# The norm behind the output projection, in two halves of the tokens

## What is computed

```python
x = x + gate[:, None, :] * jnp.einsum("bsd,de->bse", merged, w_out)
x = _rmsnorm(x, final_norm_w)        # x * rsqrt(mean(x*x) + 1e-6) * w

h = x @ pw1_w + pw1_b                # conformer_conv
a, g = jnp.split(h, 2, axis=-1)
h = a * jax.nn.sigmoid(g)
h = causal_dwconv(h, dw_w, dw_b)     # 31 taps for each channel
...
```

## Time and profile before

| | us |
|---|---|
| median of 3 runs (lowest, highest) | 2154.98 (2154.73, 2155.09) |
| the profiled execution, its own time | 2160.05 |
| its span, first to last instruction | 2158.0 |
| TensorE busy in the span | 2031.0 (94%) |
| VectorE busy | 1139.9 (53%) |
| ScalarE busy | 789.9 (37%) |
| GpSimd busy | 37.6 (2%) |

### The profile page before, as it was taken

How to read it: one execution, slowest core, us unless ns; L and a number is a source line. 1 busy time by engine, 2 the same in 40 slices (tenths; PEclk the granted TensorE clock), 3 DMA queues, 4 the chain that set the end, 5 groups by cost and what they waited for, 6 DMA issues and landing times.

```text
span 2158.0 us, 23636 instructions
## 1 busy us (share of the span) xinstructions
PE 2031.0 (94%) x9190; PEld 1621.6 (75%) x9190; DVE 1139.9 (53%) x1330; ACT 789.9 (37%) x1037; POOL 37.6 (2%) x49
## 2 busy tenths in 40 slices
PE   1998999999999899979999999989999999999996
PEld 0874678887688578668888888868777888888885
DVE  6674324225544498776455554354366745555435
ACT  2323233225522465345222232264365452222223
POOL 0000000000000000002000000020000010000000
PEclk8897999999999899989999999999999999999998
DMA  7211122221122111111222223212200222222231
GB/s 320 79 59 39 40 78 98 97 98 40 40 97 98 58 40 58 68 59 59 98 97 97 97 97 113 102 59 98 79 1 3 106 78 97 97 97 97 98 101 55
DMA packets 25861, 177.65 MB, mean 82 GB/s; under 512 B 2752, under 2 KB 4928, under 8 KB 5312
## 3 DMA queue, kind: packets, MB, share of 16 engines
q1 hardware_dynamic: 24064, 160.95, 21.8%
q10 hardware_dynamic: 1728, 15.73, 1.8%
HBM read 174.57 MB, written 2.10 MB: 82 GB/s over the span
## 4 chain that ended last, share of the span: by engine, by line
PE 85%; DVE 7%; ACT 4%; issue 1%; DMA 1%; POOL 0%; DVEq 0%; ACTq 0%; SPq 0%
PE PS L445 23%; PE PS L446 23%; PE PS L447 23%; PE PS L863 2%; PE PS L873 2%; PE PS L513 1%; PE PS L511 1%; PE PS L512 1%; PE PS L522 1%; PE PS L685 1%; DVE ADAS L1421 1%; PE PS L738 1%; DMA SWR<-w_small 1%; PE PS L688 1%; PE PS L719 1%
## 5 line engine op out<-in xcount | busy, mean ns | idle before, releaser
L445 PE MATMUL PS<-H,WH 128*128 128x512 f32 (+1 forms) x1600 | 623.3, 390 | 25.7 <-POOL L L414 12.0
L446 PE MATMUL PS<-L,WH 128*128 128x512 f32 (+1 forms) x1600 | 616.2, 385 | 0.0
L447 PE MATMUL PS<-H,WL 128*128 128x512 f32 (+1 forms) x1600 | 616.0, 385 | 0.0
L1353 DVE TENSOR_TENSOR WL<-RAW,WH 128x2048 fp32r<-128x2048 f32 x145 | 332.2, 2291 | 287.0 <-ACT WH L903 286.6
L445 PEld LDWEIGHTS PS<-H,WH 128*128 128x128 f32 x1600 | 303.5, 190 | 92.6 <-issue 19.7
L903 ACT ACTIVATE WH<-RAW 128x2048 fp32r<-128x2048 f32 x145 | 276.5, 1907 | 224.5 <-PE PS L447 179.2
L447 PEld LDWEIGHTS PS<-H,WL 128*128 128x128 f32 x1600 | 303.2, 189 | 59.9
L446 PEld LDWEIGHTS PS<-L,WH 128*128 128x128 f32 x1600 | 303.5, 190 | 58.8 <-issue 0.8
L445 PE MATMUL PS<-FH,WH 128*128 128x512 f32 (+1 forms) x376 | 142.8, 380 | 0.0
L1238 ACT ACTIVATE TT<-TT 128x512 f32<-128x512 f32 x44 | 27.8, 632 | 310.4 <-DVE TT L1932 310.4
L447 PE MATMUL PS<-FH,WL 128*128 128x512 f32 (+1 forms) x376 | 141.2, 375 | 0.0
(11 more groups left out here) (307 smaller groups left out, 2714.3 us busy)
## 6 DMA issues: line engine op xcount, KB each, us to landing
RAW<-w SPq DMA_DIRECT2D x149, 1024.0 KB, 4.9
ADA<-w_ada ACTq DMA_DIRECT2D x8, 1536.0 KB, 23.5
X<-x_t SPq DMA_DIRECT2D x1, 2048.0 KB, 14.8
PWR<-w_ple ACTq DMA_DIRECT2D x2, 1024.0 KB, 4.9
out<-X SPq DMA_DIRECT2D x8, 256.0 KB, 2.1
PR<-p_t ACTq DMA_DIRECT2D x2, 512.0 KB, 5.8
PAR<-par SPq DMA_DIRECT2D x1, 334.0 KB, 6.7
SWR<-w_small SPq DMA_DIRECT2D x1, 160.0 KB, 18.5
```

The lines of the kernel that those rows point to most:

```text
L445: nc.tensor.matmul(ps, wh, xh, start=start, stop=False, skip_group_check=skip)
L446: nc.tensor.matmul(ps, wh, xl, start=False, stop=False, skip_group_check=skip)
L447: return nc.tensor.matmul(ps, wl, xh, start=False, stop=stop, skip_group_check=skip)
L1353: v.tensor_tensor(WL[:, p], RAW[:, p], WH[:, p].bitcast(F32), ALU.subtract).then_inc(w_lo, 1)
```

## The change

The norm N_FINAL is no longer made on whole rows. `w_out` becomes a `mixed` stage with a `last_slot`, and `pw1` starts with a `first_slot`. In detail:

- During slots 1 to 3 of `w_out`, ScalarE squares the pairs of rows that are complete (`ln_squares`) and VectorE adds the squares into ACC (`squared`).
- The last slot runs tokens 0 to 255, then 256 to 511. Each half is added to X (`w_out_half`), its squares are made (`ln_half_squares`) and summed (`ln_half_sums`), one matmul of 256 columns averages over the partitions (`ln_stats` without the column of means), then come root (`rms_std`), reciprocal (`ln_recip`) and scaling (`rms_scale`) of that half.
- H is copied by pairs of rows and halves of tokens (`rms_hi`); L is made by GpSimd in the loop of L414 in place of VectorE.
- ScalarE splits the weights of `pw1`'s slot 1 between the two halves, no longer behind the norm; `pw1` is called with `split_first=False`. The load of the square root's table stands ahead of the third squaring, under slot 3.
- `LN_AFTER` gets an entry more, so that all five norms share the counters; `SHIFT_OF` and `D0` hold the counts of those that differ. Helpers used by both kinds of norm move up unchanged in what they issue.

```diff
@@ -338,11 +338,13 @@
 
         ADA_PARTS = (1, 0, 2)
 
-        N_X, N_SSM, N_FINAL, N_CONV = range(4)
+        N_X, N_SSM, N_CONV = range(3)
         LN_OF = {N_CONV: 0}
 
 
-        LN_AFTER = {"pw2": 0, "down0": 1, "wo": 2, "down1": 3}
+        LN_AFTER = {"w_out": 0, "pw2": 1, "down0": 2, "wo": 3, "down1": 4}
+        SHIFT_OF = {"pw2": 0, "down0": 1, "wo": 2, "down1": 3}
+        D0 = {"w_out": 0, "pw2": 2, "down0": 5, "wo": 8, "down1": 11}
         NP = KC // 2
         KH = 4
 
...
@@ -406,7 +408,7 @@
             select(M_SSM, ALU.is_ge, NEG, -1, 1)
             select(TRI, ALU.is_ge, 0.0, 1, -1)
 
-            for stage in ("pw2", "down0", "wo"):
+            for stage in ("w_out", "pw2", "down0", "wo"):
                 i = LN_AFTER[stage]
                 for h in range(2):
                     for p in range(NP):
@@ -528,12 +530,16 @@
                                  stop=True).then_inc(mean_ready, 1)
 
             def ln_shift(stage):
-                pe.wait_ge(s01_ready, LN_AFTER[stage] + 1)
+                pe.wait_ge(s01_ready, SHIFT_OF[stage] + 1)
                 nc.tensor.matmul(PS[:, 6, :], PAIRC.to_broadcast([P, P]), S01[:], start=True,
                                  stop=True).then_inc(m0_ps, 1)
 
             def ln_stats(stage, h):
                 pe.wait_ge(st_acc, 2 * LN_AFTER[stage] + h + 1)
+                if stage not in SHIFT_OF:
+                    nc.tensor.matmul(PS[:, 4 + h, HT:T], MEANC.to_broadcast([P, P]), ACC[:, h, 1, :],
+                                     start=True, stop=True).then_inc(lst_ps, 1)
+                    return
                 nc.tensor.matmul(PS[:, 4 + h, :], MEANC.to_broadcast([P, P]), ACC[:, h].rearrange("p a t -> p (a t)"),
                                  start=True, stop=True).then_inc(lst_ps, 1)
 
@@ -579,7 +585,7 @@
 
                 for j in range(COUNT[stage] - 1):
                     slot(Step(j), stage, units, ready if j == 0 else None,
-                         midway=(lambda: ln_shift(stage)) if j == 1 else None)
+                         midway=(lambda: ln_shift(stage)) if j == 1 and stage in SHIFT_OF else None)
                 last_slot(stage, units)
 
             pe.wait_ge(const_ready, 6)
@@ -750,8 +756,7 @@
                     turn(i - 2)
 
             gemm("att_out", ((YH, YLA), hl), (ya_lo, lambda k: k + 1))
-            gemm("w_out", ((MH, ML), (MH, ML)), (mg_lo, lambda k: k + 1))
-            norm(N_FINAL)
+            mixed("w_out", ((MH, ML), (MH, ML)), (mg_lo, lambda k: k + 1))
 
 
             def taps(s, ahead):
@@ -765,9 +770,10 @@
                 mm.then_inc(cp_ps, 1)
 
             def pw1(s):
-                first = isinstance(s.val(), int) and s.val() == 0
-                slot(s, "pw1", (hl, hl), normed(N_FINAL) if first else None)
-                if not first:
+                if isinstance(s.val(), int) and s.val() == 0:
+                    first_slot("pw1", "w_out", (hl, hl), True)
+                else:
+                    slot(s, "pw1", (hl, hl))
                     taps(s, 1)
             steps(pe, None, KC, 0, pw1, head=1)
             taps(Step(KC - 1), 0)
@@ -1108,10 +1114,51 @@
                 a(rows(MH, s.val(), 1), rows(P1, s.val(), 1), ACT.Copy).then_inc(mg_hi, 1)
 
             slots("att_out", att_out)
-            slots("w_out", lambda s, p: None)
-            act.wait_ge(bank_free, GROUP0["w_out"] + COUNT["w_out"])
-            squares(N_FINAL, X)
-            norm_hi(N_FINAL, X, H)
+            def ln_squares(stage, p):
+                i = LN_AFTER[stage]
+                if p == 0 and stage in SHIFT_OF:
+                    act.wait_ge(d_ready, D0[stage] + 1)
+                else:
+                    act.wait_ge(bank_free, GROUP0[stage] + p + 1)
+                if p:
+                    act.wait_ge(lsq_used, 3 * i + p)
+                a(SQ[:], pair(X, p), ACT.Square).then_inc(lsq_ready, 1)
+
+            def ln_half_squares(stage, h):
+                i = LN_AFTER[stage]
+                act.wait_ge(d_ready, D0[stage] + (stage in SHIFT_OF) + h + 1)
+                if h == 0:
+                    act.wait_ge(lsq_used, 3 * i + 3)
+                a(SQ[:, :, cols(h)], pair(X, NP - 1, cols(h)), ACT.Square).then_inc(lsq_ready, 1)
+
+            def rms_std(stage, h):
+                act.wait_ge(lst_ps, 2 * LN_AFTER[stage] + h + 1)
+                a(VAR[:, h], PS[:, 4 + h, HT:T], ACT.Sqrt, bias=EPS_RMS).then_inc(lstd_ready, 1)
+
+            def rms_hi(stage, h, p):
+                act.wait_ge(lt_ready, 2 * NP * LN_AFTER[stage] + NP * h + p + 1)
+                a(pair(H, p, cols(h)), pair(X, p, cols(h)), ACT.Copy).then_inc(lhi_ready, 1)
+
+            g0 = SLOT0["w_out"]
+            split_hi(Step(0), 1, g0 + 1)
+            split_hi(Step(0), 1, g0 + 2)
+            ln_squares("w_out", 0)
+            split_hi(Step(0), 1, g0 + 3)
+            ln_squares("w_out", 1)
+            split_hi(Step(0), 1, g0 + 4)
+            tables("sqrt_and_others")
+            ln_squares("w_out", 2)
+            ln_half_squares("w_out", 0)
+            rms_std("w_out", 0)
+            rms_hi("w_out", 0, 0)
+            ln_half_squares("w_out", 1)
+            rms_hi("w_out", 0, 1)
+            rms_hi("w_out", 0, 2)
+            rms_std("w_out", 1)
+            rms_hi("w_out", 0, 3)
+            split_hi(Step(0), 1, SLOT0["pw1"] + 1)
+            for p in range(NP):
+                rms_hi("w_out", 1, p)
 
             def load_ple(layer):
                 act.dma_start(PWR[:], w_ple[layer]).then_inc(ple_in, 16)
@@ -1146,7 +1193,7 @@
                 act.wait_ge(bank_free, s.val(1, GROUP0["pw1"] + 1))
                 q = s.odd()
                 a(HCH[:, q:q + 1, :], rows(HC, s.val(), 1), ACT.Copy).then_inc(hc_hi, 1)
-            slots("pw1", pw1, head=2)
+            slots("pw1", pw1, head=2, split_first=False)
             act.wait_ge(sum_ready, LN_OF[N_CONV] + 1)
             load_ple(0)
             squares(N_CONV, CV, (cen_ready, KC * LN_OF[N_CONV]))
...
@@ -1678,16 +1708,86 @@
                                 ALU.subtract).then_inc(mg_lo, 1)
             slots("att_out", att_out)
 
-            def w_out(s, p):
-                evacuated(s, "w_out")
+            halves = lambda t: t.rearrange("p (h t) -> p h t", h=2)
+
+            def squared(stage, p, start=False):
+                i = LN_AFTER[stage]
+                dve.wait_ge(lsq_ready, 5 * i + p + 1)
+                s0, s1 = halves(SQ[:, 0, :]), halves(SQ[:, 1, :])
+                sq = ACC[:, :, 1, :]
+                if start:
+                    v.tensor_tensor(sq, s0, s1, ALU.add).then_inc(lsq_used, 1)
+                    return
+                dve.wait_ge(lsq_used, 3 * i + p)
+                own.did(v.tensor_tensor(sq, sq, s0, ALU.add))
+                own.settle()
+                v.tensor_tensor(sq, sq, s1, ALU.add).then_inc(lsq_used, 1)
+
+            def ln_half_sums(stage, h):
+                i, acc_ = LN_AFTER[stage], ACC[:, h, 1, :]
+                dve.wait_ge(lsq_ready, 5 * i + 4 + h)
+                dve.wait_ge(lsq_used, 3 * i + 3)
+                own.did(v.tensor_tensor(acc_, acc_, SQ[:, 0, cols(h)], ALU.add))
+                own.settle()
+                v.tensor_tensor(acc_, acc_, SQ[:, 1, cols(h)], ALU.add).then_inc(st_acc, 1)
+
+            def ln_recip(stage, h):
+                dve.wait_ge(lstd_ready, 2 * LN_AFTER[stage] + h + 1)
+                own.did(v.reciprocal(PS[:, 4 + h, HT:T], VAR[:, h]))
+
+            def w_out(j):
+                bank = 2 * ((GROUP0["w_out"] + j) % 2)
+                dve.wait_ge(slot_done, SLOT0["w_out"] + j + 1)
                 for u in range(2):
-                    x = rows(X, s.val(2, u), 1)
-                    m = s.val(2, u + 2 * KC)
-                    g = ADAV[:, m:m + 1] if isinstance(m, int) else ADAV[:, bass.ds(m, 1)]
-                    ins = v.scalar_tensor_tensor(x, PS[:, 2 * p + u:2 * p + u + 1, :], g, x, ALU.mult, ALU.add)
-                free(s, "w_out", ins)
-            slots("w_out", w_out)
-            norm_out(N_FINAL, X, X, lambda m: col("final_norm_w", m), H, L)
+                    m = 2 * j + u
+                    ins = v.scalar_tensor_tensor(X[:, m, :], PS[:, bank + u, :], ADAV[:, 2 * KC + m:2 * KC + m + 1],
+                                                 X[:, m, :], ALU.mult, ALU.add)
+                ins.then_inc(bank_free, 1)
+
+            def w_out_half(h):
+                if h == 0:
+                    dve.wait_ge(half_done, LN_AFTER["w_out"] + 1)
+                else:
+                    dve.wait_ge(slot_done, SLOT0["w_out"] + COUNT["w_out"])
+                for u in range(2):
+                    m = 2 * NP - 2 + u
+                    ins = v.scalar_tensor_tensor(X[:, m, cols(h)], PS[:, last_bank("w_out") + h, cols(u)],
+                                                 ADAV[:, 2 * KC + m:2 * KC + m + 1], X[:, m, cols(h)], ALU.mult, ALU.add)
+                ins.then_inc(d_ready, 1)
+
+            def rms_scale(h, p):
```

(54 more changed lines are left out.)

32 lines of the change are left out of this document (5 added, 27 removed).

## The result

The changed kernel takes 2138.28 us, the median of four executions (2136.45 to 2144.61), against 2154.86 for the kernel before (2154.68 to 2155.09) beside it on the same chip: a ratio of 0.9927, 95% interval 0.9914 to 0.9939. It is 0.7% faster, by 13.1 to 18.5 us. The profiled execution took 2144.61 us, the longest of the four, with a span of 2142.9 (before: 2160.05 and 2158.0).

A forecast was written before the change was run, and what follows sets the result against it. It took the serial norm walk, then ScalarE's copies, diagonals and sigmoid, taps and weights, as the bound at this boundary. 17.25 - 1.3 - 0.4 = 15.55 us; 2154.98 - 15.6 = 2139.4 us, 80% range 2136.5 to 2143.

The forecast's parts named there:

- the two deductions: Taken off the diagonals' gain: 1.3 us for a low TensorE clock, 0.4 us for low parts waiting on GpSimd.
- The chain: From `w_out` into `pw1`: norm, end of ScalarE's H copies, diagonals, sigmoid, taps, slot 2's weights; not TensorE's start.
- The clock term: Before `pw1`'s first product: idle of 2.4 us lowers TensorE's clock, second half's chain 1.3 us later (0 to 1.6).
- The low parts' term: At the taps' weights: VectorE's low part waits for GpSimd's L, 0.4 us (bounds 0 and 1.3).
- 17.25: Diagonals at 731.25 instead of 748.50, 17.25 us earlier: norm and copies 15.9, moved split 1.9, less 0.5.
- 15.55: Net gain at the diagonals after deductions, 17.25 - 1.3 - 0.4 us, going through to the end.
- the moved split: ScalarE's weight split for `pw1`'s slot 1, moved from behind the norm: 1.9 us, less 0.5 for an uncovered low part.
- B: Rival: GpSimd's eight L operations at 2.98 us each pace `pw1`'s slot 0; 8.9 us won, 2146.1; 7%.
- C: Rival: clock holds before `pw1`'s first product and before slot 2; 17.25 us plus 1.5 more, 2136.2; 6%.
- D: Rival: clock stays low from 718.65 through `pw1`'s slots 0, 1 and taps; 4.8 us later, 2159.8; 2%.
- E: Rival: no change; second half's late statistics inside `pw1`'s first slot hold TensorE and ScalarE, 11 to 15 us; 5% with overlooked causes.

The follow-up runs named there:

- the whole first slot: Changed kernel with only the halving of `pw1`'s first slot undone, both statistics ahead of it; 2142.25 us, 0.9945 of the kernel before.
- the moved weights: Changed kernel with both parts of the taps' weights made during `w_out`'s second slot, not behind the norm; 2139.79 us, 0.9930 of the kernel before.
- the split back: Changed kernel with ScalarE's weight split for `pw1`'s slot 1 back behind the norm, ahead of the diagonals; 2141.08 us, 0.9935 of the kernel before.
- the sigmoid between the diagonals: Changed kernel with slot 0's sigmoid and its copy after 13 of the 26 diagonals; 2136.03 us, 0.9911 of the kernel before.
- the filled kernel: Changed kernel plus unread products: 18 ahead of `pw1`'s first slot, 9 behind slot 0's taps; 2139.34 us, 0.9926 of the kernel before.
- the first of the two combinations: Changed kernel with taps' weights moved to `w_out`'s second slot and second half's squares summed by TensorE; 2133.83 us, 0.9909 of the kernel before.

## Why the prediction was right, and which terms of it were not

Predicted 2139.4, measured 2138.28, and 2139.55 over all 15 executions. With the marker at 706.80 as in the prediction, its walk stands beside what came (the rows of after less 1.32):

| step | predicted | measured |
|---|---|---|
| half 0's adds begin | 712.5 | 712.49 |
| statistics matmul, half 0 | 715.3 | 715.17 |
| its reciprocal ends | 718.1 | 718.07 |
| first product of `pw1` | 721.1 | 721.14 |
| idle before it | 2.4 | 2.52 |
| second half's sums end | 721.8 | 722.86 |
| second half's reciprocal ends | 725.4 | 726.46 |
| last H copy ends | 729.3 | 730.39 |
| diagonals begin, before the two deductions | 731.25 | 733.32 |
| idle before slot 2 | 3 | 2.56 |

**The chain was read rightly.** Diagonals, slot 2 and the stretch moved by 15.18, 15.16 and 15.14. That it is ScalarE's row of copies and diagonals, and not TensorE's start, was tested from both sides: 8.4 us on TensorE's start alone moved slot 2 by 3.3 and the stretch by 1.6 (the whole first slot), while diagonals 1.62 and 2.03 us earlier made the stretch 3.2 and 2.04 shorter, and diagonals 5.71 later made it 4.1 longer. The clock before slot 2 makes the 1.6 between 1.62 and 3.2 and between 5.71 and 4.1.

**The clock term (1.3) was mis-sized: it is 0.** I put the 2.4 us of idle beside the 2.59 behind which the clock was low. Behind 2.51 or 2.52 us there it held at 1.00 in the kernel after, its two repeats, the moved weights and the split back. In one more kernel with the same norm and an idle of 2.51 it fell, the sigmoid between the diagonals: 1.4 us behind the first product, for some 3.2 us. That kernel's window, and rows of its timeline:

```profile
719.10:722.30 3.20, 3.20 (x13) 2.80 (x13) 2.92 (x6) 2.09 (x4) 1.40 (x3) 0.50 0.02 5
```

```profile
719.44 1.22 PE L540 MATMUL PS<-ACC,COLS 128*128 128x256 f32 x2
...
720.21 0.63 ACT L1140 ACTIVATE H<-X 128x512 fp32r<-128x512 f32 x1 [2.46 <-DVE X L1768]
...
720.74 0.46 ACT L1136 ACTIVATE VAR<-PS,COLS 128x256 f32<-128x256 f32 x1
```

Its statistics matmul took 1.22 us and not 0.70, yet the root started 17.41 behind the marker, as in the kernel after, and the diagonals at 26.54 against 26.52. In ScalarE's list the copy of the first half's third pair stands ahead of that root, and it waits for a scaling that stands behind the two sums in VectorE's list. So in the kernel after the second half's chain runs through these lists, and the matmul that my term priced has some 0.6 us to spare. What a fall right at the first product would cost, as I had assumed it, no run shows.

**The low parts' term (0.4) was mis-sized: it is 2.07,** and half of it was at a place I hadn't looked at. I allowed for GpSimd holding VectorE only at the taps' weights. There it cost 1.0 (1.26 for 0.27). But two of the second half's sums run beside L as well, 0.82 and 1.55 in place of 0.42 and 0.43: together they lose 1.52, began some 0.5 earlier than my walk had them, and end 1.06 later; that went through the scalings behind them, root, reciprocal and copies to the diagonals. L on VectorE shows the cause, the sums on TensorE and the moved weights show that both places lie on the chain. The rule of the Trainium skill that the prediction quoted (SBUF — State Buffer, Who interferes with whom) would have put 1.3 us at the taps' weights, where 1.0 came, and by it the two sums had to be counted too. The traces agree with it: each of the three operations lost time beside an L (0.39, 1.13 and 0.99 us), and none with GpSimd silent.

The two errors are of opposite sign: 17.25 - 0 - 2.07 = 15.18 against 15.55. The near hit of the sum is partly that, and so partly luck. The near hit of the time is too: the three sets of executions of this kernel have medians of 2138.28, 2142.32 and 2140.38, against a forecast of 2139.4.

**Inside the 17.25** I put 1.9 to the moved split less 0.5 for a low part no longer covered, 1.4. Moved back alone it costs 0.38, and that is no third error: the 1.0 that GpSimd adds to this low part is counted above, and 1.4 - 1.0 = 0.4. With L on VectorE the diagonals start 0.63 us behind the start of the copy of the taps' weights, and before the change 2.01 behind it, with the split between them; the difference is the 1.4.

**What the two halvings give.** Without the one in `w_out` the diagonals lose 5.71 of 15.18. Without the one in `pw1`'s first slot they lose nothing (26.42), slot 2 loses 3.3 and the stretch 1.6. The other 9.5 us at the diagonals I didn't take apart further: in it are the squares and the table load moved under slots 0 to 3, the averaging matmuls down from 16 to 4, and the split reciprocal.

**The rivals.** B: an L takes 1.27 beside VectorE's reciprocals and scalings, and 1.77 on average (7.06 for four) even when a weight split lies beside; under the 2.1 from which B decides. C came half true in the kernel after: the clock held before the first product but not before slot 2, where holding is worth 1.66 us (the filled kernel). D: no low clock from 718 to 726. E: no idle before either statistics matmul.

**From the stretch to the whole.** The two profiled spans differ by 15.1: 1.32 longer up to the marker, 15.14 shorter in the stretch, then 1.94 longer up to the first copy of `q1`'s results (QHH), and 3.22 shorter from there to the end. In the other kernels, all with the same code there, these last two lengths are 558.4 to 560.5 and 726.4 to 729.2 (before 558.70 and 729.93, after 560.64 and 726.71). Whether the change has a hand in that remainder of -1.3 us stays open; with a single profile of the kernel before it can't be told from the spread.

## What to carry to other kernels

Find the instruction that the next stage really waits for, here the diagonals on ScalarE, and count every edit by what it does to that one; TensorE's own start could move 8.4 us, and the next slot that mattered moved 3.3. When an operation is given to GpSimd, list every two-input VectorE operation that will run beside it and is on the chain, also small ones of 0.3 us, and price each at up to an L's length. When executions spread by 9 us and edits are worth 2, measure from a marker just ahead of the edit to one behind it; when the chain has been shortened until TensorE is the bound, more of the same gives little (0.44 us where it gave 4.46 alone).

## What the hardware showed that I had not expected

An idle of nearly one length had both outcomes for the clock. Before slot 2 it was 2.56 to 2.59 us in the kernel before, in the kernel after and its repeats, with the sums on TensorE and with L on VectorE, and the clock fell; with the split back it was 2.78 and it fell; with `w_out`'s last slot undivided it was 2.58 and the clock held. Before the first product of `pw1` it was 2.51 or 2.52 in six profiles; in five the clock held, in one it fell. The low clock before slot 2 was worth 1.6 us in the three comparisons that show its price, so a change that shortens such an idle by 2 us can be paid double, as the moved weights were (3.2 for 1.62). Inside `pw1`'s first slot the fall cost the diagonals 0.02 us.

Most of the spread of the executions comes from code that no variant touched. The marker lay between 702.43 and 708.25 us in the profiles. One place where they part is far ahead of it, from 186 to 206 us. There the clock was 0.77 and 0.80 in the kernel after and in the one with the sums on TensorE, whose markers came at 708.12 and 707.07. It was 1.00 in the two with the earliest markers, L on VectorE (702.77) and the first of the two combinations (702.43), whose window shows 101 products in place of 82:

```profile
186.00:206.00 20.00, 19.89 (x101) 11.70 (x99) 8.68 (x11) 3.60 (x6) 0.00 (x0) 1.00 0.25 89
```

The other profiles fit in between: of all 14, the kernel before among them, the higher the clock in this window, the earlier the marker. Why the clock falls there in one execution and not in another the runs don't tell.
